# A mixture-of-experts down product in rounded parts: three single-pass products in place of one in full float32

## The reference, cut to what matters

```python
def _moe(h, router_w, router_bias, w_gate, w_up, w_down):
    ...
    for e in range(N_EXPERTS):
        he = jax.nn.silu(h @ w_gate[e]) * (h @ w_up[e])
        y = y + comb[:, e:e + 1] * (he @ w_down[e])
    return y
```

## Time and profile before

| | |
|---|---|
| median of three runs | 1384.85 us |
| the profiled execution | 1382.05 us |
| its span | 1380.1 us |
| PE, DVE, ACT, POOL busy | 84%, 59%, 31%, 12% of the span |
| PE instructions of the down product (line 1556) | 368, 176.6 us |
| DVE subtractions for WL (line 1187) | 208, 244.7 us |

### The profile page before, as it was taken

How to read it: one execution, slowest core, us unless ns; L and a number is a source line. 1 busy time by engine, 2 the same in 40 slices (tenths; PEclk the granted TensorE clock), 3 DMA queues, 4 the chain that set the end, 5 groups by cost and what they waited for, 6 DMA issues and landing times.

```text
span 1380.1 us, 14989 instructions
## 1 busy us (share of the span) xinstructions
PE 1154.0 (84%) x4661; PEld 810.8 (59%) x4662; DVE 819.2 (59%) x966; ACT 433.9 (31%) x536; POOL 163.1 (12%) x126
## 2 busy tenths in 40 slices
PE   4969998539998989928999999969994499889992
PEld 1553445336665656626888888838873466556661
DVE  4775736456988767745444444453655567667773
ACT  5130112124444444443111111131221245344551
POOL 2000000031222212200000000000000022213221
PEclk9989999859999999959999999979996599999996
DMA  8548712407998988650133333430224368999855
GB/s 347 183 183 287 273 49 107 183 23 248 317 342 262 286 288 279 161 170 16 46 107 107 107 106 106 167 137 31 92 92 183 136 225 238 300 295 293 255 116 152
DMA packets 81614, 251.62 MB, mean 182 GB/s; under 512 B 8604, under 2 KB 33380, under 8 KB 72676
## 3 DMA queue, kind: packets, MB, share of 16 engines
q1 hardware_dynamic: 60180, 182.86, 35.1%
q0 software_dynamic: 17056, 50.40, 15.9%
q10 hardware_dynamic: 4336, 17.83, 3.4%
HBM read 220.65 MB, written 46.14 MB: 193 GB/s over the span
## 4 chain that ended last, share of the span: by engine, by line
PE 66%; DVE 13%; DMA 10%; ACT 4%; issue 4%; ACTq 1%; DVEq 1%; SPq 1%; POOL 0%; POOLq 0%; PEldq 0%
PE PS L1539 12%; PE PS L1556 11%; PE PS L1636 7%; PE PS L1471 6%; PE PS L1640 6%; PE PS L1637 6%; PE PS L1446 5%; DMA RAW<-in_moe_w_up_dram 4%; DMA WDR<-in_moe_w_down_dram 3%; DVE ACC L862 2%; PE PS L1483 2%; PE PS L1384 2%; PE PS L1529 2%; DVE WL L1187 2%; ACT WH L685 2%
## 5 line engine op out<-in xcount | busy, mean ns | idle before, releaser
L1187 DVE TENSOR_TENSOR WL<-RAW,WH 128x1024 fp32r<-128x1024 f32 x208 | 244.7, 1221 | 46.3 <-ACT WH L685 45.7
L685 ACT ACTIVATE WH<-RAW 128x1024 fp32r x208 | 202.6, 1046 | 110.0 <-issue 80.4
L1556 PE MATMUL PS<-WDR,HET 128*128 x368 | 176.6, 624 | 27.2 <-DVE HET L1172 21.9
L1539 PE MATMUL PS<-WH,XTH 128*128 128x512 f32 x384 | 172.7, 450 | 12.3 <-issue 7.2
L1636 PE MATMUL PS<-HTH,WINH 128*128 128x512 f32 x384 | 153.5, 400 | 5.4 <-DVE HTL L1297 5.4
L1539 PE MATMUL PS<-WL,XTH 128*128 128x512 f32 x384 | 154.6, 403 | 0.0
L1539 PE MATMUL PS<-WH,XTL 128*128 128x512 f32 x384 | 154.6, 403 | 0.0
L1637 PE MATMUL PS<-HTL,WINH 128*128 128x512 f32 x384 | 150.5, 392 | 0.0
L1556 PEld LDWEIGHTS PS<-WDR,HET 128*128 128x128 f32 x368 | 68.8, 197 | 107.9 <-issue 107.9
L862 DVE SCALAR_TENSOR_TENSOR ACC<-WA,SC,ACC 128x1024 f32<-128x1024 f32 (+1 forms) x88 | 113.0, 1284 | 18.1 <-DMA WA<-in_w_ada_dram 13.3
L1640 PE MATMUL PS<-HTH,WINL 128*128 128x512 f32 x384 | 120.8, 395 | 0.0
(11 more groups left out here) (194 smaller groups left out, 1384.8 us busy)
## 6 DMA issues: line engine op xcount, KB each, us to landing
WA<-in_w_ada_dram SPq DMA_DIRECT2D x36, 1024.0 KB
RAW<-in_moe_w_gate_dram SPq DMA_DIRECT2D x32, 1024.0 KB
RAW<-in_moe_w_up_dram SPq DMA_DIRECT2D x32, 1024.0 KB
WDR<-in_moe_w_down_dram SPq DMA_DIRECT2D x32, 1024.0 KB
WINR<-in_conv_w_in_dram SPq DMA_DIRECT2D x24, 512.0 KB, 3.8
x_dram<-X POOLq DMA_DIRECT2D x16, 512.0 KB, 2.9
h_dram<-H SPq DMA_DIRECT2D x16, 512.0 KB, 2.6
WA<-in_w_ada_dram ACTq DMA_DIRECT2D x8, 1024.0 KB
```

The lines of the kernel that those rows point to most:

```text
L685: nc.scalar.activation(piece_of(WH[par], i), raw_piece(e, i), ACT.Copy).then_inc(w_high, 1)
L1187: V.tensor_tensor(piece_of(WL[par], i), raw_piece(e, i), piece_of(WH[par], i).bitcast(f32), ALU.subtract).then_inc(w_low, 1)
L1539: ins = T.matmul(bank(2), x[:, ch, :], w[par][:, :, ch, :], start=ch == 0 and i == 0, stop=ch == NC - 1 and i == 2)
L1556: ins = T.matmul(bank(4 + h), HET[par][:, f, :], WD[:, f, h * BANK:(h + 1) * BANK], start=f == 0, stop=f == FF // P - 1)
```

## The change

The down product becomes three products of rounded parts, HETH·WDH + HETH·WDL + HETL·WDH, like the gate and up products. Four tiles are added (WDH and WDL, 128x2x1024 each; HETH and HETL, 128x2x128 each) and HET goes. All four have a single buffer.

- ACT writes HETH from PSUM and WDH in two halves (`down_high`, in front of its slot). It waits there for the transposes of the hidden tile, for the down product of the slot before (which frees WDH) and for the weights.
- DVE writes HETL (in place of the copy HET) and the first half of WDL, at the head of its body.
- POOL writes the second half of WDL (`down_low`), in front of its gather and scatter. It has not done arithmetic in this loop so far.
- PE transposes the hidden tile of s-1 ahead of gate_up(s), and down(s-1) stays at the slot's end. The down product is now in halves: the first waits for DVE's half of WDL, the second for POOL's.
- Two of the four pieces of WH and WL are now made one slot later than the other two (one slot ahead of use in place of two). Their order in the loop bodies changes on ACT and DVE.
- The expert's number is read into a register once more (ACT: three reads for a slot in place of one; DVE: three in place of one; POOL: one in place of none; PE: none in place of one).

```diff
+        def down_low(layer, s):
+            f, b = FF // P - 1, layer * MAX_SLOTS
+            e = pool.value_load(SEID[0:1, ds(s, 1)], min_val=0, max_val=EXPERTS - 1)
+            pool.wait_ge(wd_high, s * (FF // P) + (b * (FF // P) + f + 1))
+            nc.gpsimd.tensor_tensor(WDL[:, f], down_part(e, f), WDH[:, f].bitcast(f32), ALU.subtract).then_inc(wd_low[f], 1)
+
         def slot(layer, s):
+            down_low(layer, s)
             if s < MAX_SLOTS - 4:
                 pool.wait_ge(xt_tr, s + (layer * MAX_SLOTS + 3))
                 gather(layer, s + 4, s % 2)
...
+            def down_high(s):
+                e = act.value_load(SEID[0:1, ds(s, 1)], min_val=0, max_val=EXPERTS - 1)
+                act.wait_ge(he_tr, s + (b + 1))
+                nc.scalar.activation(HETH[:].rearrange("p f n -> p (f n)"), bank(3)[:, 0:FF], ACT.Copy).then_inc(het_high, 1)
+                act.wait_ge(yd_mm, s + b)
+                act.wait_ge(down_in[0], even_loaded(e, layer, 16))
+                act.wait_ge(down_in[1], odd_loaded(e, layer, 16))
+                for f in range(FF // P):
+                    nc.scalar.activation(WDH[:, f], down_part(e, f), ACT.Copy).then_inc(wd_high, 1)
...
             def slot(s, par):
+                down_high(s - 1)
+                weights_high(s + 1, 1 - par, (2, 3))
                 gate(s)
                 xt_high(s + 1)
-                weights_high(s + 2, par)
+                weights_high(s + 2, par, (0, 1))
...
-            def heT_evac(s, par):
-                dve.wait_ge(he_tr, s + (b + 1))
-                V.tensor_copy(HET[par][:].rearrange("p f n -> p (f n)"), bank(3)[:, 0:FF]).then_inc(heT_ready, 1)
+            def het_split(s):
+                dve.wait_ge(het_high, s + (b + 1))
+                V.tensor_tensor(HETL[:].rearrange("p f n -> p (f n)"), bank(3)[:, 0:FF],
+                                HETH[:].rearrange("p f n -> p (f n)").bitcast(f32), ALU.subtract).then_inc(het_low, 1)
+
+            def down_low(s, e):
+                for f in range(FF // P - 1):
+                    dve.wait_ge(wd_high, s * (FF // P) + (b * (FF // P) + f + 1))
+                    V.tensor_tensor(WDL[:, f], down_part(e, f), WDH[:, f].bitcast(f32),
+                                    ALU.subtract).then_inc(wd_low[f], 1)
...
             def body(s, par, free=True):
-                e = expert_of(s + 2)
-                heT_evac(s - 1, 1 - par)
+                e0, e1, e2 = expert_of(s - 1), expert_of(s + 1), expert_of(s + 2)
+                het_split(s - 1)
+                down_low(s - 1, e0)
+                weights_low(s + 1, 1 - par, e1, (2, 3))
                 gated(s, par)
                 xt_low(s + 1)
-                weights_low(s + 2, par, e, (0, 1))
+                weights_low(s + 2, par, e2, (0, 1))
                 y_evac(s - 1, 1 - par, free)
-                weights_low(s + 2, par, e, (2, 3))
...
+            def down(s):
+                pe.wait_ge(het_high, s + (b0 + 1))
+                pe.wait_ge(het_low, s + (b0 + 1))
+                last = FF // P - 1
+                for f in range(FF // P):
+                    pe.wait_ge(wd_low[f], s + (b0 + 1))
+                    for i, (x, w) in enumerate(((HETH, WDH), (HETH, WDL), (HETL, WDH))):
+                        for h in range(2):
+                            ins = T.matmul(bank(4 + h), x[:, f, :], w[:, f, h * BANK:(h + 1) * BANK],
+                                           start=f == 0 and i == 0, stop=f == last and i == 2)
                 ins.then_inc(yd_mm, 1)
 
             def slot(s, par, next_nth, more=True, last=False):
 
                 pe.wait_ge(he_ready, s + b0)
+                hidden_transposes(s - 1, 1 - par)
                 if not last:
                     gate_up(s, par)
-                hidden_transposes(s - 1, 1 - par)
                 if more:
                     transposes(s + 1, 1 - par, next_nth)
                 pe.wait_ge(yo_ready, s + (b0 - 1))
-                down(s - 1, 1 - par)
+                down(s - 1)
```

More of the change, by code:

```diff
@@ L194, in backbone @@
     XTH = r.put("XTH", [P, NC, P], f32r)
-    assert r.at <= base + width(X.shape) + 2 * width(XS[0].shape)
+    WDH = r.put("WDH", [P, FF // P, D], f32r)
+    WDL = r.put("WDL", [P, FF // P, D], f32r)
+    assert r.at <= base + width(X.shape) + 2 * width(XS[0].shape) + 3 * D * 4
     r = Region(ada_at - width(SQ.shape))
     HE = [r.put(f"HE{i}", [P, FF]) for i in range(2)]
-    HET = [r.put(f"HET{i}", [P, FF // P, P]) for i in range(2)]
+    HETH = r.put("HETH", [P, FF // P, P], f32r)
+    HETL = r.put("HETL", [P, FF // P, P], f32r)
     assert r.at <= ada_at
@@ L264, in backbone @@
     down_in = [sem(f"down_in{i}") for i in range(2)]
-    w_high, w_low = sem("w_high"), sem("w_low")
+    w_high, w_low, het_high, het_low = sem("w_high"), sem("w_low"), sem("het_high"), sem("het_low")
+    wd_high, wd_low = sem("wd_high"), [sem(f"wd_low{f}") for f in range(FF // P)]
     x_stored = [sem(f"x_stored{i}") for i in range(2)]
@@ L678, in xt_high, with weights_high @@
                                      ACT.Copy).then_inc(xt_act, 1)
-            def weights_high(s, par):
+            def weights_high(s, par, pieces=range(PIECES)):
                 e = act.value_load(SEID[0:1, ds(s, 1)], min_val=0, max_val=EXPERTS - 1)
-                act.wait_ge(raw_in[0], even_loaded(e, layer, 32))
-                act.wait_ge(raw_in[1], odd_loaded(e, layer, 32))
-                for i in range(PIECES):
+                if 0 in pieces:
+                    act.wait_ge(raw_in[0], even_loaded(e, layer, 32))
+                    act.wait_ge(raw_in[1], odd_loaded(e, layer, 32))
+                for i in pieces:
                     nc.scalar.activation(piece_of(WH[par], i), raw_piece(e, i), ACT.Copy).then_inc(w_high, 1)
+            def down_high(s):
[7 more added lines that the diff above has]
+                    nc.scalar.activation(WDH[:, f], down_part(e, f), ACT.Copy).then_inc(wd_high, 1)
             def gate(s):
@@ L710, in _ @@
             xt_high(1)
[L711 removed]
+            weights_high(2, 0, (0, 1))
             if layer == 0:
@@ L1238, in pair_if_used @@
                 with dve.Else():
-                    dve.wait_ge(w_low, 2 * PIECES * i + (b + 3) * PIECES)
-                    for sig in (heT_ready, he_ready, xt_dve, yo_ready):
+                    dve.wait_ge(yo_ready, 2 * i + b)
+                    for sig in (het_low, he_ready, xt_dve, yo_ready, wd_low[0]):
                         dve.sem_inc(sig, 2)
@@ L1256, in _ @@
                 for s in (MAX_SLOTS - 2, MAX_SLOTS - 1, MAX_SLOTS):
-                    par = s % 2
-                    heT_evac(s - 1, 1 - par)
+                    e0 = expert_of(s - 1)
+                    het_split(s - 1)
+                    down_low(s - 1, e0)
+                    if s + 1 < MAX_SLOTS:
+                        weights_low(s + 1, 1 - s % 2, expert_of(s + 1), (2, 3))
                     if s < MAX_SLOTS:
-                        gated(s, par)
+                        gated(s, s % 2)
                     if s + 1 < MAX_SLOTS:
                         xt_low(s + 1)
-                    y_evac(s - 1, 1 - par)
+                    y_evac(s - 1, 1 - s % 2)
             with dve.Else():
-                dve.wait_ge(w_low, 2 * PIECES * PAIR_LOOPS + (b + 3) * PIECES)
-                dve.sem_inc(heT_ready, 3)
+                dve.wait_ge(yo_ready, 2 * PAIR_LOOPS + b)
+                for sig in (het_low, wd_low[0]):
+                    dve.sem_inc(sig, 3)
+                dve.sem_inc(w_low, 2)
                 dve.sem_inc(he_ready, 2)
@@ L1546, in hidden_transposes @@
                 ins.then_inc(he_tr, 1)
-            def down(s, par):
-                e = pe.value_load(SEID[0:1, ds(s, 1)], min_val=0, max_val=EXPERTS - 1)
-                pe.wait_ge(heT_ready, s + (b0 + 1))
-                pe.wait_ge(down_in[0], even_loaded(e, layer, 16))
-                pe.wait_ge(down_in[1], odd_loaded(e, layer, 16))
-                WD = WDR[:, ds(e & 1, 1)].rearrange("p r f n -> p (r f) n")
-                for h in range(2):
-                    for f in range(FF // P):
-                        ins = T.matmul(bank(4 + h), HET[par][:, f, :], WD[:, f, h * BANK:(h + 1) * BANK],
-                                       start=f == 0, stop=f == FF // P - 1)
+            def down(s):
[8 more added lines that the diff above has]
+                                           start=f == 0 and i == 0, stop=f == last and i == 2)
                 ins.then_inc(yd_mm, 1)
@@ L1576, in _ @@
             pe.wait_ge(he_ready, 1 + b0)
+            hidden_transposes(0, 0)
             gate_up(1, 1)
-            hidden_transposes(0, 0)
             transposes(2, 0, 2)
-            down(0, 0)
+            down(0)
             slot(2, 0, 2)
```

25 lines of the change are left out of this document (18 added, 7 removed).

## The result

The changed kernel takes 1413.54 us (median of 4 runs, 1411.80 to 1416.91), the kernel before 1384.48 beside it (4 runs, 1380.87 to 1386.57): ratio 1.0228, 95% interval 1.0204 to 1.0252. It is slower, and the time is the predicted one to 1 us.

The account below looks back on a forecast made before the run. The prediction took PE to bound ordinary slots and DVE the adaLN slots. Adding +21 us (adaLN), +6 (ordinary) and +4 (refills), together +31, to the profiled 1382.05 us gave 1413 us, range 1376 to 1445.

Parts of the forecast that it names:

- the likeliest of the cases: The forecast itself: POOL and DVE interfere, with a POOL subtraction of 2.2 us; own range 1397 to 1440 us, chance 0.55.
- PE's wait behind the sixth product of twelve: Sign of the forecast: in the down product PE idles between sixth and seventh instruction, released by POOL.
- a POOL subtraction over 3 us: Sign that would refute the forecast's size; POOL's subtraction for the second half of WDL was taken as 2.2 us.
- adaLN slots: Eight slots with an adaLN block on DVE, which bounds them: from 11.2 to 13.8 us each, +21 us together.
- The hold: In an adaLN slot POOL's subtraction holds off DVE's WDL for some 1.7 of its 2.2 us.
- Ordinary slots: 28 slots bound by PE at 10.5 us before: 10.7 us each after the change, +6 us together.
- the loop through POOL: Two-slot loop: YO, scatter, POOL's subtraction, second half of down, gate and up, next YO; 19.9 us, 21.1 with interference.
- POOL's subtraction: POOL making the second half of WDL: taken as 2.2 us, with 0.87 and 2.61 as the ends.
- The rule on exclusion: A DVE instruction with two SBUF inputs and a GpSimd instruction reading SBUF exclude each other; the second waits out the first.
- Refills: Four places where PE waits for an expert's weights: RAW freed later, each grows by 1 us, +4 together.
- PE's slot: PE's work in an ordinary slot: from 10.49 to 9.58 us, 0.91 less, if nothing else is late.
- No interference: Rival: no interference, POOL's loop eats the gain; adaLN slots 12.1, ordinary 10.1 us, no change at 1382; chance 0.20.

Follow-up runs that it names:

- e3: Changed kernel with DVE's WL and WDL subtractions replaced by products with zero whose second operand lies in PSUM, not SBUF: 1372.52 us, ratio 0.9941 to before.
- e4: Changed kernel with POOL subtracting only 512 of the 1024 columns of its half and DVE the other 512: 1408.03 us, ratio 1.0181 to before.
- e2: Changed kernel with DVE's WL and WDL subtractions replaced by products with zero, second operand still in SBUF: 1415.34 us, ratio 1.0234 to before.
- e6: Kernel before plus one idle POOL subtraction per slot, behind the scatter, whose result nobody reads: 1403.89 us, ratio 1.0164 to before.
- e5: Kernel before with only the hidden transposes moved in front of the gate and up product: 1367.19 us, ratio 0.9907 to before.
- e10: Second measurement, in more rounds, of the kernel before with only the hidden transposes in front of gate and up: 1371.25 us, ratio 0.9932.
- e1: Changed kernel with DVE subtracting both halves of WDL and POOL doing DMAs only: 1382.31 us, ratio 0.9989 to before.
- e7: Changed kernel with POOL copying its half of the raw down weights into WDL instead of subtracting: 1371.91 us, ratio 0.9936 to before.
- e8: Changed kernel with POOL subtracting into a spare tile nobody waits for, PE using WDL's first half twice: 1391.47 us, ratio 1.0077 to before.
- e9: Kernel before with the hidden transposes moved behind the token transposes, directly in front of the down product: 1404.10 us, ratio 1.0170 to before.

## Why the prediction was right, and which of its terms were not

The outcome (slower, by 29 us), the cause (POOL and DVE subtracting at once, DVE the one that pays) and the likeliest of the cases held. Of its signs, PE's wait behind the sixth product of twelve and the stretched WL and WDL were seen; a POOL subtraction over 3 us was not the rule (median 2.96, longest 3.41). Against the profiled runs:

- **adaLN slots**, predicted +21, measured 108.0 - 92.9 = +15.1. Without interference 12.1 was predicted, and e3 has 98.9 / 8 = 12.4 with the refill in it, 12.0 to 12.2 in the undisturbed slots. The hold was taken as 1.7 and is 2.49 - 1.21 = 1.3. And two of the eight intervals also waited for weights before (13.04 and 12.84): they grew by 0.8 in all, where the sum charged 2.6 for each, as the longer slot took in the wait. By the same double count the prediction has 28 ordinary intervals; there are 30, of which the table leaves out the first.
- **Ordinary slots**, predicted 10.7 with a range of 10.4 to 11.2, measured 11.3: +23.3 in place of +6. This is the step that failed. I had DVE's sum (8.9 us of 9.6) and I had the hold, but I charged the hold to the loop through POOL, at 1.2 us for a turn of the loop, which is two slots, and never added it to DVE's own sum: 8.9 + 2.2 would have been 11.1. The order of the two engines was wrong as well. I had POOL ready 3.2 us behind YO's end, during the second WL, so that 1.6 us of it would lie beside HE and XTL. In the trace it starts 1310.09 - (1306.42 + 1.28) = 2.4 us behind it, as the first WL ends, and the second has to stand still for the rest; DVE works in order, so HE and XTL, which could have run beside POOL, stand behind it. PE feels both: in the 29 ordinary slots it idles 22.5 us for DVE's XTL and 13.7 us for POOL's WDL.
- **POOL's subtraction**, taken as 2.2 us with 2.61 as the upper end, is 2.96. Three passes at the rate of the memset was no bound from above. The Trainium skill ("GPSIMD Engine Reference", Performance versus the Vector engine) would give an estimate of 2.25 by half of its figure; the trace disagrees by 0.7. By e4's 1.86 for 512 columns an estimate of 2 x 1.86 - 2.96 = 0.76 us doesn't shrink with the columns.
- **The rule on exclusion** of the Trainium skill ("SBUF — State Buffer", Who interferes with whom) was weighed as undecided. e2 and e3 bear it out with 43 us, and e6, in whose ordinary slots POOL met operations with a PSUM operand or idle time, shows its other side. The rule of the Trainium skill has the one that issues first win. In e4's rows WL starts at 1294.67, 0.41 ahead of POOL, and is held all the same; the starts in the records don't tell who wins. In all 46 cases of the changed kernel DVE was the one that waited.
- **Refills**, predicted +4, measured 73.9 - 82.1 = -8.2. Longer slots give a load of weights more time before it is waited for. The six intervals exceed six ordinary ones of their own kernel by 24 to 26 us at slots of 10.0 to 10.1 (e3, e5, e10), by 19 at 10.2 to 10.5 (e1, before, e6), by 12 to 14 in e2, e7, e8 and e9 (10.4 to 11.4), and by 6 and 4 in the changed kernel and e4 (11.3). A few long intervals elsewhere (13.56 and 13.54 in e4, 13.81 in e7, 12.94 in e8) are counted as ordinary and blur this by a microsecond or so. The direction is shown; why e2 and e9, whose slots are as long, keep twice the wait isn't. It is a give-back, and faster slots lose it: in its profiled run e5 won 10 us in ordinary slots and lost 4 here.
- **PE's slot**, predicted as 9.58, is 9.48 in e3 and e8 where nothing holds DVE up, so the gain is 10.49 - 9.48 = 1.01. It isn't all the three products'. "The moved hidden transposes cost the same 0.22" left out what they give: 10.49 - 10.12 = 0.37 comes from their place alone (e5), and 0.64 from the new form of the product (3.44 in e5, 2.80 in e3's chain). The place of the transposes was costed at nothing.
- **No interference**, the rival at 1382, is nearly the world that e3 built: ordinary 291.2 / 29 = 10.04 (predicted 10.1), adaLN 12.1 (predicted the same), and 1372.5 us in all. The prediction's loop through POOL is real there: what lies above PE's 9.48 is for the most part PE's wait for POOL's WDL, 10.9 us in 14 of the 29 slots. Once DVE is held, DVE's sum lies above the loop. Of the 12 us between the two profiled runs (1382.05 and 1369.86), 6 lie inside the two mixture loops (adaLN +6.0, ordinary -13.4, refills +2.3, the first interval -1.0) and 6 in parts of the program that the change doesn't touch. e1, which escapes the interference by leaving POOL out, comes to the same time as before.

The three terms (adaLN, ordinary, refills) were off by -6, +17 and -12 us, which nearly cancel. The time to 1 us is luck; the sign and the cause are not.

What stays open: whether a subtraction on POOL could be put into the stretch of DVE's order that e6 found free, and still be in time for the product. It wasn't tried as a kernel; the late subtraction in e8, which nobody waited for, shows only that the place is cheap. Nor was the new product with all low parts on DVE given an order of its own (e1 keeps the changed one).

## What to carry to other kernels

Work given to a second engine is a loss if the two exclude each other and the first is nearly full: write the held time into the busy sum of the engine that is held, and compare that sum with the slot, as well as looking at the loops. Where an engine works in order, what it stands still on delays what could have run. And take a change apart: its smallest part, two lines moved so that a hand-over through another engine is covered, was worth 0.7 to 0.9%, and the rest more than used it up.
